# Two fp32 transformer blocks on one core: a weight split between two tap halves, early tiles behind the first level, projections kept by group, and a group's loads in four portions

## The reference, cut to what matters

```python
# D = 2048, S = 256, fp32 throughout
def conv_ffn(h, w_up, conv_w, conv_b, w_down):       # block "B": D_FF = 5632
    u = h @ w_up                                      # 2048 -> 11264
    c = conv_b + sum(shift(u, 2 - i) * conv_w[i] for i in range(3))
    gate, val = split(c, 2)
    return (gelu(gate) * val) @ w_down

def odd_layer(x, ...):                                # block "D", 32 heads of 64
    r, k, v, g = xr @ w_r, xk @ w_k, xv @ w_v, xg @ w_g
    w_log = -softplus(-(w0 + tanh(xw @ w1) @ w2)) - 0.5
    a = sigmoid(a0 + (xa @ a1) @ a2)
    kk = normalised(k * k_k); k = k * (1 + (a - 1) * k_a)
    # per head: state = state * decay - (state kk)(kk a)^T + v k^T ; o = state r
    o = wkv7_scan(r, decay, k, v, kk, a)
    o = group_norm(o) * gn_w + gn_b + sum(r * k * r_k) * v
    return (o * silu(g)) @ w_o
```

## Time and profile before

| | |
|---|---|
| median of 3 runs | 2585.29 us (2583.71 to 2595.74) |
| the profiled execution's own time | 2580.39 us |
| its span, first to last instruction | 2578.6 us |
| mean granted PE clock | 0.984 |
| PE / PEld / DVE / ACT / POOL busy | 2468.6 / 2054.3 / 1494.5 / 1253.2 / 179.2 us |
| block B, rounds of the up product | about 700 to 1190 us |
| block D, pipeline over the groups | about 2220 to 2480 us |

### The profile page before, as it was taken

How to read it: one execution, slowest core, us unless ns; L and a number is a source line. 1 busy time by engine, 2 the same in 40 slices (tenths; PEclk the granted TensorE clock), 3 DMA queues, 4 the chain that set the end, 5 groups by cost and what they waited for, 6 DMA issues and landing times.

```text
span 2578.6 us, 38999 instructions
## 1 busy us (share of the span) xinstructions
PE 2468.6 (96%) x15976; PEld 2054.3 (80%) x15976; DVE 1494.5 (58%) x1964; ACT 1253.2 (49%) x1656; POOL 179.2 (7%) x208
## 2 busy tenths in 40 slices
PE   8999999999999999999999999999899999989897
PEld 6886888888788878787888788878788888778775
DVE  5457554574566566666444544445667555678666
ACT  5446444564555555554444444534445445555443
POOL 2002000000000000000000100000000001134320
PEclk9999999999999999999999999999999999899998
DMA  8756666655555555456555555535466677323352
GB/s 251 246 168 146 202 202 204 199 184 191 196 175 176 187 185 184 160 187 244 191 191 191 188 192 183 167 110 177 161 210 211 220 226 255 100 50 90 95 197 98
DMA packets 242409, 463.41 MB, mean 180 GB/s; under 512 B 9952, under 2 KB 39849, under 8 KB 240480
## 3 DMA queue, kind: packets, MB, share of 16 engines
q1 hardware_dynamic: 223488, 422.08, 49.5%
q0 software_dynamic: 18464, 39.22, 5.4%
q10 hardware_dynamic: 320, 0.13, 0.0%
HBM read 446.66 MB, written 14.74 MB: 179 GB/s over the span
## 4 chain that ended last, share of the span: by engine, by line
PE 46%; DVE 5%; ACT 2%; issue 1%; POOL 0%; ACTq 0%; DVEq 0%
PE bank L331 12%; PE bank L333 12%; PE bank L332 12%; PE bank L2117 2%; DVE d_products L2087 1%; PE bank L357 1%; PE bank L358 1%; PE bank L359 1%; PE bank L1958 1%; PE bank L2518 1%; PE bank L2214 1%; PE bank L2187 1%; PE bank L1599 0%; DVE d_steps L2136 0%; PE bank L482 0%
## 5 line engine op out<-in xcount | busy, mean ns | idle before, releaser
L268 DVE TENSOR_TENSOR w_low<-raw,w_high 128x1024 fp32r<-128x1024 f32 x768 | 928.9, 1220 | 825.1 <-ACT w_high L262 824.1
L262 ACT ACTIVATE w_high<-raw 128x1024 fp32r<-128x1024 f32 x768 | 805.0, 1057 | 943.2 <-PE bank L333 911.1
L331 PE MATMUL bank<-w_high,b_h_high 128*128 128x512 f32 x704 | 278.2, 395 | 8.8 <-DVE w_low L268 7.5
L333 PE MATMUL bank<-w_high,b_h_low 128*128 128x512 f32 x704 | 275.1, 391 | 0.0
L332 PE MATMUL bank<-w_low,b_h_high 128*128 128x512 f32 x704 | 275.0, 391 | 0.0
L331 PE MATMUL bank<-w_high,a_h_high 128*128 128x512 f32 (+1 forms) x640 | 247.5, 387 | 2.3 <-DVE w_low L268 2.3
L333 PE MATMUL bank<-w_high,a_h_low 128*128 128x512 f32 (+1 forms) x640 | 246.2, 385 | 0.0
L332 PE MATMUL bank<-w_low,a_h_high 128*128 128x512 f32 (+1 forms) x640 | 246.1, 385 | 0.0
L331 PE MATMUL bank<-w_high,c_x_high 128*128 128x512 f32 x512 | 203.3, 397 | 0.7 <-DVE c_x_low L505 0.7
L332 PE MATMUL bank<-w_low,c_x_high 128*128 128x512 f32 x512 | 200.3, 391 | 0.0
L333 PE MATMUL bank<-w_high,c_x_low 128*128 128x512 f32 x512 | 200.1, 391 | 0.0
(11 more groups left out here) (372 smaller groups left out, 3718.1 us busy)
## 6 DMA issues: line engine op xcount, KB each, us to landing
raw<-in_w_up SPq DMA_DIRECT2D x88, 1024.0 KB, 5.1
raw<-in_w_in SPq DMA_DIRECT2D x76, 1024.0 KB, 5.2
raw<-in_ev_w_in SPq DMA_DIRECT2D x48, 1024.0 KB, 5.1
raw<-in_w_down SPq DMA_DIRECT2D x44, 1024.0 KB, 5.0
raw<-in_w_out SPq DMA_DIRECT2D x16, 1024.0 KB, 5.0
raw<-in_ev_w_out SPq DMA_DIRECT2D x16, 1024.0 KB, 5.0
raw<-in_od_w_r SPq DMA_DIRECT2D x16, 1024.0 KB, 5.0
raw<-in_od_w_k SPq DMA_DIRECT2D x16, 1024.0 KB, 5.1
```

The source lines that it names most:

```text
L262: act.activation(wh[n % 4][:, :, 0:width], raw_half, ACT.Copy).then_inc(sem("w_high_made"), 1)
L268: vec.tensor_tensor(wl[n % 4][:, :, 0:width], raw_half, wh[n % 4][:, :, 0:width].bitcast(F32), ALU.subtract).then_inc(sem("w_low_made"), 1)
L331: pe.matmul(b, xh, wh[n][:, k % 2, 0:width], start=(c == 0 and k == 0), stop=False)
L333: mm = pe.matmul(b, xl, wh[n][:, k % 2, 0:width], start=False, stop=(c == j.chunks - 1 and k == 3))
```

## The change

The low part of the first unit of the next panel is made between the two halves of the gate taps; `split_early` and all of the identities but the first two tiles move into the pipeline of group 0 (halves 3 and 5); `rkvg` is stored as [group, partition, r/k/v/g, row half, 256 columns], so that a load of one kind and group is 128 pieces of 2 KB and not 256 of 1 KB; `group_rows` issues k and its row first, then waits for steps 1T, 2Y and 2T of group n - 2 before the next portions.

```diff
@@ -1431,18 +1431,18 @@
         low(0)
-        gate(1, True)
+        per = 2 * j.looped * j.chunks
+        gate(1, True, lambda: split_units(vec, False, j, 2 * per, 1))
         with vec.Fori(2, ROUNDS) as i:
-            panel(i, 0)
+            split_units(vec, False, j, 1, per // 2 - 1, i)
 ...
             low(i - 1)
-            gate(i, True)
+            gate(i, True, lambda: split_units(vec, False, j, per, 1, i))
         jd = plan["down"]
-        split_units(vec, False, jd, 0, 1)
@@ -1759,7 +1759,7 @@
     dl = [at(f"d_low{i}", [128, KT, S], F32R, PH + 64 + 32 * i) for i in range(2)]
-    DS = [at(f"d_staged{i}", [128, 2, PANEL], F32, PH + 112 + 4 * i) for i in range(2)]
+    DS = [at(f"d_staged{i}", [128, 2, 2, PANEL // 2], F32, PH + 112 + 4 * i) for i in range(2)]
@@ -1767,8 +1767,8 @@
-    RKVG = [[at(f"d_{n}{i}", [128, 2, GW], F32, (PH, PH + 8, 0)[i] + 2 * k) for k, n in enumerate("rkvg")]
-            for i in range(3)]
+    RKVGS = [at(f"d_rkvg{i}", [128, 4, 2, GW], F32, (PH, PH + 8, 0)[i]) for i in range(3)]
+    RKVG = [[RKVGS[i][:, k, :, :] for k in range(4)] for i in range(3)]
@@ -1814,7 +1814,7 @@
     XKEPT2 = x_kept2.rearrange("(t p) d -> p t d", p=128)
-    kept = dram("rkvg", [4, S, D])
+    kept = dram("rkvg", [GROUPS, 128, 4, 2, GW])
@@ -1879,17 +1879,29 @@
         def load_kept(k, what):
-            load(RKVG[n % 3][k][:, :, :], kept[k].rearrange("(t p) d -> p t d", p=128)[:, :, cols], what)
+            load(RKVG[n % 3][k][:, :, :], kept[n, :, k, :, :], what)
 ...
             await_step(sp, "prep_vec", "bonus_sum", n - 2)
-        for k, name in enumerate(ROW_NAMES[:GNW]):
-            load(ROWS[n % 2][:, k, :], rows_of(name)[cols].partition_broadcast(128), "group")
-        for k in (0, 1):
-            load_kept(k, "group")
+
+        def load_row(k):
+            load(ROWS[n % 2][:, k, :], rows_of(ROW_NAMES[k])[cols].partition_broadcast(128), "group")
+        load_kept(1, "group")
+        load_row(KK)
+        if n >= 2:
+            await_step(sp, "level_pe", "1T1", n - 2)
+        load_row(W0)
+        load_row(A0)
+        if n >= 2:
+            await_step(sp, "level_pe", "2Y1", n - 2)
+        load_kept(0, "group")
+        if n >= 2:
+            await_step(sp, "level_pe", "2T1", n - 2)
+        load_row(KA)
+        load_row(RK)
@@ -1898,7 +1910,7 @@
         cols = slice(GW * n, GW * n + GW)
-        sp.dma_start(RKVG[n % 3][3][:, :, :], kept[3].rearrange("(t p) d -> p t d", p=128)[:, :, cols]
+        sp.dma_start(RKVG[n % 3][3][:, :, :], kept[n, :, 3, :, :]
@@ -2131,7 +2143,7 @@
                 await_step(vec, "level_pe", f"{k}Y{t}", n)
-                if n == 0 and t == 0 and k <= 2:
+                if n == 0 and t == 0 and k <= 4:
@@ -2332,11 +2344,13 @@
-    def pipeline(eng, level, state, prep, post, score, first, last, ahead, behind):
+    def pipeline(eng, level, state, prep, post, score, first, last, ahead, behind, begin):
 ...
                     level(eng, n, (half + 1) // 2, "TY"[half % 2])
+                if n == 0:
+                    begin(eng, half)
@@ -2459,8 +2473,9 @@
             gp.wait_ge(sem("acc_free"), plan["odd_" + GEMMS[k]].p0 + p + 3)
-            gp.dma_start(kept[k].rearrange("(t p) d -> p t d", p=128)[:, :, PANEL * p:PANEL * p + PANEL],
-                         DS[p % 2][:, :, :]).then_inc(sem(f"rkvg_stored{p % 2}"), 16)
+            gp.dma_start(kept[2 * p:2 * p + 2, :, k, :, :].rearrange("g q t c -> q g (t c)"),
+                         DS[p % 2][:, :, :, :].rearrange("q g t c -> q g (t c)")
+                         ).then_inc(sem(f"rkvg_stored{p % 2}"), 16)
@@ -2500,7 +2515,7 @@
                 gp.dma_start(X[:, :, :], XKEPT2).then_inc(sem("x_back2"), 16)
-        pipeline(gp, idle, idle, prep_pool, post_pool, idle, idle, last, POOL_AHEAD, POOL_BEHIND)
+        pipeline(gp, idle, idle, prep_pool, post_pool, idle, idle, last, POOL_AHEAD, POOL_BEHIND, idle)
@@ -2540,7 +2555,7 @@
         prep_pe(pe, 1, 1)
-        pipeline(pe, level_pe, state_pe, prep_pe, idle, score_pe, idle, last, PE_AHEAD, PE_BEHIND)
+        pipeline(pe, level_pe, state_pe, prep_pe, idle, score_pe, idle, last, PE_AHEAD, PE_BEHIND, idle)
@@ -2591,16 +2606,24 @@
                         prep_act(act, 0, part)
-            run_act(act, plan["odd_" + name], lambda p, t: DS[p % 2][:, t, :], free, post, each,
+            run_act(act, plan["odd_" + name], lambda p, t: DS[p % 2][:, :, t, :], free, post, each,
 ...
         act.wait_ge(sem("w_used"), 2 * plan["odd_out"].g0)
-        for rows in (slice(0, 2), slice(2, 10)):
-            act.activation(STEPS_I[:, rows, :, :].rearrange("p a h s -> p (a h) s"),
-                           ident_b.unsqueeze(1).to_broadcast([128, 4 * (rows.stop - rows.start), 64]), ACT.Copy
+
+        def fill_steps(k, stop):
+            act.activation(STEPS_I[:, 2 * k - 2:2 * stop, :, :].rearrange("p a h s -> p (a h) s"),
+                           ident_b.unsqueeze(1).to_broadcast([128, 8 * (stop - k + 1), 64]), ACT.Copy
                            ).then_inc(sem("steps_filled"), 1)
-            if rows.start == 0:
+
+        def begin(act, half):
+            if half == 3:
+                fill_steps(2, 2)
                 split_early(act, True)
+            if half == 5:
+                fill_steps(3, 3)
+                fill_steps(4, 5)
+        fill_steps(1, 1)
@@ -2610,7 +2633,7 @@
                 split_units(act, True, jo, half - 6, 1)
-        pipeline(act, level_act, state_act, prep_act, post_act, idle, idle, last, ACT_AHEAD, ACT_BEHIND)
+        pipeline(act, level_act, state_act, prep_act, post_act, idle, idle, last, ACT_AHEAD, ACT_BEHIND, begin)
@@ -2690,7 +2713,10 @@
             first_turned(vec, 0, t)
-        split_early(vec, False)
+
+        def begin(vec, half):
+            if half == 3:
+                split_early(vec, False)
@@ -2699,7 +2725,7 @@
         pipeline(vec, level_vec, state_vec, prep_vec, post_vec, score_vec, first_level, last, VEC_AHEAD,
-                 VEC_BEHIND)
+                 VEC_BEHIND, begin)
```

## The result

| | before | after |
|---|---|---|
| median of 6 runs | 2586.14 us (2583.71 to 2595.74) | 2571.47 us (2568.29 to 2577.20) |
| profiled execution, its own time | 2580.39 us | 2572.22 us |
| span | 2578.6 us | 2570.4 us |

The ratio is 0.9939, 95% interval 0.9926 to 0.9951: 14.7 us faster by the medians, where 16.7 was forecast, and 2571.47 where 2569 was. Timed again in other rounds the changed kernel stood at 0.9943 (0.9931 to 0.9955). Rival (a), by which the loads change nothing, had put the gain at 12.7 us; the measured one lies halfway between it and the forecast, so the time alone doesn't choose between them.

What follows compares the result with a forecast made beforehand. PE, busy 2468.6 of 2578.6 us, was taken as the bound, with gains only from its standstill or low clock. 10 + 2.7 + 4 = 16.7 us off 2580.4 gives 2563.7, as a median 2569 us; range 2559 to 2577.

Steps and rivals of the forecast that it cites:

- Rival (a): Block D: group loads change nothing for PE, issue waits stay or only move; gain 12.7 us, 2572.6 us; chance 0.25.
- block B: Low part between the gate taps: nine PE waits for w_low go, 7.5 us idle plus restart cost, 10 us gained.
- The second unit: Block B: its low part is ready at 814.9, PE wants it at 815.5; 0.6 us in hand, so no new wait.
- the tenth wait: Block B, first units of w_down: 0.76 us behind another tap group that is not touched, so it stays.
- Start of the pipeline: Block D: fills and early unit behind the first level bring step 3T closer to 1Y; 2.7 us, bounds 0 and 5.
- Rival (c): Block D: later first burst makes its own stall, up to 2.75 us, plus 2 us low clock; 2573.4 us; chance 0.10.
- Rows kept by group: Loads of r, k, v, g in half the pieces: a group's four loads take 2.9 us and not 3.6; stores cost nothing.
- Four portions: Block D group loads: only order changes for groups 4 to 7, group 3 is spread; 4 us from fewer issue stalls.
- The sum: Whole kernel: 10 + 2.7 + 4 = 16.7 us gained, 2569 us as a median.

Runs made afterwards that it cites:

- e1: Kernel before with only the low part made between the two halves of the gate taps; ratio 0.9963, 9.6 us.
- e3: Kernel before with only rkvg kept by group (2 KB pieces), loads in the old order; ratio 1.0001.
- e7: Changed kernel with loads of groups 5 to 7, all but g, bringing 8 of 256 columns; these iterations take 28.8 us, without issue waits.
- e8: Changed kernel with the portions let go at later steps that SP has not yet passed (2T, 3Y, 3T, 4Y); ratio 0.9926, median 2562.65 us.
- e9: Kernel e8 with the early unit of w_o split ahead of the pipeline, as before the change; ratio 0.9930, median 2563.98 us.
- e10: Kernel e9 with one more wait, for step 5Y, ahead of v, its norm rows and g; ratio 0.9928, median 2563.60 us.
- a0: The changed kernel itself, unaltered, timed once more in other rounds; ratio 0.9943 of before.
- e2: Kernel before with only the fills and the early unit moved behind the first level; ratio 0.9999, 0.3 us.
- e5b: Changed kernel without the four portions: old order of loads, no added waits, timed beside the changed kernel; ratio 0.9955.

## Why the prediction was right, and which term was not

- **What bounds, and block B.** Right in place, price and cover. 10.3 us in the trace, 9.6 timed, 10 forecast; the restart cost that was added to the idle figure (7.5 us idle, 10.3 lost) is borne out. The second unit was not late, and the tenth wait stayed.
- **Start of the pipeline.** The mechanism was right (3T closer to 1Y, moved fills in the gaps), the size low: 3.67 us where 2.7 was taken. ACT reached its reading of PE's sums (L1995) 8.3 us after 1Y; the forecast had 8.4. What came faster was the rest, 5.7 us from there to 3T where before it was 6.6: the two halves of 2T had reached ACT 0.85 us apart (2232.64 and 2233.49) with PE at its low clock and now lay ready together, which saved 0.55 us, and DVE's chain to the next copy took 3.0 us and not 3.4.
- **What that is worth at the end** was overrated. Alone it gave 0.3 us, between 2.8 faster and 2.6 slower; in the kernels with this start the gain up to the second iteration is anything from 1.1 to 3.4 us and hangs on whether the late first burst makes its issue wait. Rival (c), 0.10, happened in the profiled execution, with a wait of 2.27 us where 2.75 and a low clock were priced.
- **Rows kept by group.** Nothing in the time. The 0.7 us less of DMA time per burst that was worked out from two windows with different loads is not shown: e1 and e3 differ in piece size and have nearly the same share (39.6 and 40.6%), and executions of one kernel differ by more.
- **Four portions.** This is the weak step: "I take a third of 12, 4 us". The prediction itself had found that for groups 4 to 7 the waits are met before SP gets there, and credited the mere order. In the traces order gave nothing: only group 3's wait of 1.0 to 1.8 us (3.34 once) went, and the sum of the issue waits, 11.3 and 8.7 us, is not below the 10.5 and 7.9 of before and e1, whose block D is as before. That is rival (a) in all but group 3. The timed worth of 3 us, with an interval from nothing to over 5, doesn't refute the 4, but no wait in the traces accounts for it beyond group 3's. That the waits come from the bytes of the group loads was right (e7), and what really parts the loads removes more than half of them (e8).
- **The sum** came within 2 us because block B's term was 60% of it and right. For the rest there is luck in it: timed alone, the start gave 0.3 us for 2.7 and layout with portions 2.8 for 4, which with block B's 9.6 makes 12.7 us, the value of rival (a). The whole kernel gained 14.7; the parts' intervals, some 3 us to either side each, cover the difference, but nothing shows where it comes from.

Open: why the kernels with spread portions are 5 to 10 us shorter over the pipeline in their traces and only 3.5 us faster by their medians (a part of it is the choice of execution: the profiled ones of e8, e9 and e10 lie 1.7, 3.7 and 2.3 us below their medians, that of a0 1.1 us); what PE waits for in an issue wait; and why e2, with a first iteration that is 2.1 us shorter, times as before. The issue waits vary from one execution to the next by about as much as is to be explained, and one trace per kernel doesn't settle it.

## What to carry to other kernels

A weight split, or any short instruction that the bound engine needs next, belongs between the pieces of a longer group on its engine, and what a wait costs is read from start to start and not from its idle figure. Before a load is given a wait to spread it, look when its queue gets there: a wait that is met already spreads nothing, and only times at which the queue stands show a gap. Where many small matrix instructions run beside bulk loads, an "issue" wait may come from those loads; try it by shrinking the bytes and nothing else. And before a few per cent between two traces are put down to a change, hold them against two executions that don't have it.

## What the runs showed of the hardware that was not expected

- PE stood still behind group loads, for up to 3.3 us, although the instruction queue moved only 36 packets of 16 KB in the 212 us of the pipeline; in the iterations whose loads had lost nearly all their bytes (e7) there was no such wait.
- These waits differ between two executions of one kernel: in the changed one 2.27 and 0.32 us at one place, 11.3 and 8.7 us in total.
- So does the time that DMA engines take for the same loads: 2.16 MB in the same 1808 packets took 41.9% and 35.7% of 20 us (60 to 80 us after 1Y) in the two executions of the changed kernel, and 51.8% in e5b.
- DVE instructions of one size (128x512) took quite different times on the start's chain: L2048 1.51 us before and its like (L2060) 0.83 after, L2057 0.68 before and its like (L2069) 1.16 after. POOL was busy beside all of them but L2057, and also beside L2063, which took 0.68, so a busy POOL alone doesn't decide it.
